# Rotary embedding in a two-layer streaming encoder: tables scaled by the norm, and another order of the mixing steps

## The reference, cut to what matters

```python
def rmsnorm(x, g):
    xf = x.astype(jnp.float32)
    y = xf * lax.rsqrt(jnp.mean(xf * xf, axis=-1, keepdims=True) + EPS)
    return (y * g.astype(jnp.float32)).astype(x.dtype)

def rope(x, pos):
    ...
    x1, x2 = xf[..., :half], xf[..., half:]
    return jnp.concatenate([x1 * cos - x2 * sin, x2 * cos + x1 * sin], axis=-1).astype(x.dtype)

def token_mix(z, pos, ws, bs, sink, g_q, w_uq, w_uk, w_uv, g_kv, cache):
    u, va, q, k, vb, cq, ckv_raw, kpe_raw = split_proj(z)
    q = rope(q.reshape(B, T, B_HEADS, B_HEAD_DIM), pos)
    k = rope(k.reshape(B, T, B_KV_HEADS, B_HEAD_DIM), pos)
    ...
    b = swa_prompt(q, k, vb, sink)
    c_lat = mla_prompt(q_lat, q_pe, ckv, kpe)

def layer(h, pos, cache, ...):
    h = ffn_half(h, n1, w1g, w1u, w1d)
    z = rmsnorm(h, nm) @ w_in
    m, st = token_mix(z, pos, ...)
    h = h + m @ w_out
    h = ffn_half(h, n2, w2g, w2u, w2d)
```

## Time and profile before

| | us |
|---|---|
| median of 3 runs (2272.84 to 2275.41) | 2273.33 |
| the profiled execution, its own time | 2275.03 |
| span of the profiled execution | 2273.0 |
| busy in the span: PE, DVE, ACT, POOL | 2214.6, 693.7, 676.1, 755.9 |
| mixing of the first layer, from `z:v` to the last output step | 454 to 696 |
| mixing of the second layer, the same stretch | 1573.6 to 1815.6 |

### The profile page before, as it was taken

How to read it: one execution, slowest core, us unless ns; L and a number is a source line. 1 busy time by engine, 2 the same in 40 slices (tenths; PEclk the granted TensorE clock), 3 DMA queues, 4 the chain that set the end, 5 groups by cost and what they waited for, 6 DMA issues and landing times.

```text
span 2273.0 us, 41807 instructions
## 1 busy us (share of the span) xinstructions
PE 2214.6 (97%) x16519; PEld 2147.2 (94%) x16519; DVE 693.7 (31%) x993; ACT 676.1 (30%) x1074; POOL 755.9 (33%) x324
## 2 busy tenths in 40 slices
PE   8999999998998999999999999999989999999999
PEld 7999999997778999999999999999977799999999
DVE  5222211146646222221122222112555462222211
ACT  5222222224434222222232222222244342222222
POOL 3334343431022433343433433334311133333331
PEclk9999999999998999999999999999999999999999
DMA  4322222331111323223222232324211022322232
GB/s 121 91 75 83 83 86 77 105 88 41 51 47 38 93 74 92 74 79 92 80 76 82 77 89 74 93 76 119 61 45 53 29 75 74 92 74 87 75 91 86
DMA packets 344052, 176.16 MB, mean 77 GB/s; under 512 B 36848, under 2 KB 339152, under 8 KB 343952
## 3 DMA queue, kind: packets, MB, share of 16 engines
q1 hardware_dynamic: 341872, 171.15, 26.5%
q10 hardware_dynamic: 2080, 3.67, 0.5%
HBM read 171.17 MB, written 3.62 MB: 77 GB/s over the span
## 4 chain that ended last, share of the span: by engine, by line
PE 91%; DVE 5%; issue 2%; ACT 2%; DMA 0%; SPq 0%; DVEq 0%; ACTq 0%
PE pair L879 85%; DVE sq_sum L1193 1%; PE pair L1071 1%; PE pair L1057 1%; PE pair L1079 1%; PE pair L1011 1%; DVE top L1379 1%; PE pair L1049 1%; PE pair L1062 0%; ACT probs L785 0%; DVE rms_q L1327 0%; DVE rms_kv L1321 0%; PE pair L1094 0%; DMA raw<-in_w_up_dram 0%; PE pair L896 0%
## 5 line engine op out<-in xcount | busy, mean ns | idle before, releaser
L618 POOL TENSOR_TENSOR w_low<-raw,w_high 128x1024 fp32r<-128x1024 f32 (+1 forms) x320 | 755.7, 2379 | 1489.2 <-ACT w_high L643 1489.2
L879 PE MATMUL pair<-x_high,w_high 128*128 128x288 f32 x3296 | 712.1, 298 | 4.7 <-DVE h L1435 2.8
L879 PE MATMUL pair<-x_low,w_high 128*128 128x288 f32 x3296 | 707.6, 296 | 0.0
L879 PE MATMUL pair<-x_high,w_low 128*128 128x288 f32 x3296 | 707.4, 296 | 0.0
L879 PEld LDWEIGHTS pair<-x_high,w_high 128*128 128x128 f32 x3296 | 533.1, 189 | 8.2 <-DVE x_low L1187 3.0
L879 PEld LDWEIGHTS pair<-x_low,w_high 128*128 128x128 f32 x3296 | 533.0, 189 | 0.0
L879 PEld LDWEIGHTS pair<-x_high,w_low 128*128 128x128 f32 x3296 | 532.8, 189 | 0.0
L643 ACT ACTIVATE w_high<-raw 128x1024 fp32r<-128x1024 f32 (+1 forms) x322 | 318.3, 1023 | 233.6 <-DMA raw<-in_w_down_dram 151.1
L879 PE MATMUL pair<-hidden_high,w_high 128*128 128x288 f32 x1408 | 301.6, 296 | 0.0
L879 PE MATMUL pair<-hidden_low,w_high 128*128 128x288 f32 x1408 | 301.5, 296 | 0.0
L879 PE MATMUL pair<-hidden_high,w_low 128*128 128x288 f32 x1408 | 301.4, 296 | 0.0
(11 more groups left out here) (183 smaller groups left out, 1377.0 us busy)
## 6 DMA issues: line engine op xcount, KB each, us to landing
raw<-in_w_up_dram SPq DMA_DIRECT2D x90, 512.0 KB, 3.8
raw<-in_w_gate_dram SPq DMA_DIRECT2D x88, 512.0 KB, 4.1
raw<-in_w_down_dram SPq DMA_DIRECT2D x64, 512.0 KB, 3.6
raw<-in_w_down_dram SPq DMA_DIRECT2D x32, 384.0 KB, 3.3
raw<-in_w_in_dram SPq DMA_DIRECT2D x20, 512.0 KB, 3.9
raw<-in_w_in_dram SPq DMA_DIRECT2D x16, 256.0 KB, 3.6
raw<-in_w_out_dram SPq DMA_DIRECT2D x8, 512.0 KB, 3.7
raw<-in_w_out_dram SPq DMA_DIRECT2D x16, 256.0 KB, 3.9
```

The source lines that it names most:

```text
L618: nc.gpsimd.tensor_tensor(**low_of(s, slot_size(s))).then_inc(low_ready, 1)
L879: mm = nc.tensor.matmul(ps[p][:, half, 0:HALF], w, x[:, half * HALF:(half + 1) * HALF], start=first and k == 0 and q == 0, stop=last and k ...
```

## The change

The norm and the rotary tables are both factors for each position, so they are multiplied with each other once a layer: `sin64` and `cos64` become sin x rms and cos x rms, in place, in the DVE part of `z:k`. A rotated tile then takes three passes: z = PSUM x sin64 (what the half swap reads), dst = PSUM x cos64, and, behind the half swap on PE, dst = PSUM + dst. The multiplication by sin goes ahead of the half swap, which is right since both halves of a head have the same sines. The PSUM pair of a rotated projection is now emptied by two passes.

`PLAN` is another list: the same steps in another order, with other pairs. The buffer of `probsT` is now taken by the step's turn in the list (`buffer_of`), which in this list gives each step the buffer that its number gave before.

```diff
-PLAN = """w:q0 z:k@0 sumx@3 w:q1 z:v@1 tw@2 w:q2 z:q0@0 w:q3 w:va0 w:va1 rot:k@3 tc@2 z:q1@1 rot:q0@3 z:q2@0 rot:q1@3 tv@1
...
+PLAN = """w:q0 z:k@0 sumx@3 w:q1 z:v@1 tw@2 w:q2 z:q0@0 w:q3 w:va0 rot:k@2 w:va1 tc@1 rot:q0@3 w:u0 z:q1@0 tv@3 z:q2@2
...
-    n = {"z": 1, "sumx": 1, "sumkv": 2, "sumq": 1, "tw": 1, "rot": 3, "a": 4, "qp": 1, "qn": 1,
+    n = {"z": 4 if arg == "k" else 2 if step in ROTATED else 1, "sumx": 1, "sumkv": 2, "sumq": 1, "tw": 1, "rot": 3 if arg in ("kpe", "qp") else 1, "a": 4, "qp": 1, "qn": 1,
...
 def evacuated(step):
 
     kind, arg = split(step)
+    if step in ROTATED:
+        return "vector", vector_end(step)
...
+def buffer_of(step):
+
+    kind, arg = split(step)
+    turn = [s for s in MIX if split(s)[0] in ("T", "MT")]
+    return turn.index({"T": "T", "O": "T", "MT": "MT", "MO": "MT"}[kind] + f":{arg}") % 2
...
                             nc.vector.reciprocal(rms[:, :], rms[:, :]).then_inc(rms_ready, 1)
                             dve.wait_ge(rms_ready, 3 * layer + 2)
+                            dve.wait_ge(mix_in, layer * N_MIX_IN + MIX_IN_FIRST)
+                            emit(nc.vector.tensor_tensor(sin64[:, :], sin64[:, :], rms[:, :], ALU.mult), names[0])
+                            emit(nc.vector.tensor_tensor(cos64[:, :], cos64[:, :], rms[:, :], ALU.mult), names[1])
+                            own(names[1])
...
-                        emit(nc.vector.tensor_tensor(rows2(dst), halves(p), rows2(rms), ALU.mult), names[0])
+                        if step in ROTATED:
+                            emit(nc.vector.tensor_tensor(rows2(dst), halves(p), rows2(sin64), ALU.mult), names[-2])
+                            emit(nc.vector.tensor_tensor(rows2(roped[arg]), halves(p), rows2(cos64), ALU.mult), names[-1])
+                        else:
+                            emit(nc.vector.tensor_tensor(rows2(dst), halves(p), rows2(rms), ALU.mult), names[0])
...
+                        if arg in roped:
+                            pe_did(dve, layer, step)
+                            own(vector_end(f"z:{arg}"))
+                            emit(nc.vector.tensor_tensor(rows2(roped[arg]), halves(p), rows2(roped[arg]), ALU.add), names[0])
+                            continue
```

More of the change, by code:

```diff
@@ L103 @@
 MLA_TILES = [1, 3, 4, 2, 0]
-PLAN = """w:q0 z:k@0 sumx@3 w:q1 z:v@1 tw@2 w:q2 z:q0@0 w:q3 w:va0 w:va1 rot:k@3 tc@2 z:q1@1 rot:q0@3 z:q2@0 rot:q1@3 tv@1
[L105 to L112, removed]
+PLAN = """w:q0 z:k@0 sumx@3 w:q1 z:v@1 tw@2 w:q2 z:q0@0 w:q3 w:va0 rot:k@2 w:va1 tc@1 rot:q0@3 w:u0 z:q1@0 tv@3 z:q2@2
+rot:q1@1 z:q3@0 rot:q2@2 z:va0@1 w:u1 w:ckv w:cq0 rot:q3@2 z:va1@1 tva:0@2 S:0@3 z:u0@0 T:0@1 w:cq1 tva:1@2 S:1@3
+z:u1@0 tk@2 a:0@1 T:1@3 O:0@0 S:2@2 z:ckv@3 a:1@2 w:cq2 w:kpe T:2@3 S:3@2 z:cq0@0 O:1@0 T:3@1 S:4@3 sumkv@2 O:2@3
+T:4@0 S:5@1 z:cq1@2 z:cq2@3 O:3@2 T:5@0 w:qn w:A0 S:6@1 z:kpe@3 sumq@2 vc:0@0 O:4@3 T:6@0 rep@1 S:7@2 tckv@1 qp@3
+rot:kpe@0 O:5@2 T:7@3 S:8@0 tkpe@1 qn:0@2 O:6@3 A:0@0 w:A1 T:8@2 w:B0 S:9@1 qn:1@3 A:2@2 O:7@0 T:9@1 ql:0@3
+ql:1@2 O:9@0 A:5@1 rot:qp@0 A:1@2 vc:1@1 O:8@0 w:B1 ql:2@2 MS:0@1 ql:3@0 A:7@3 A:6@2 A:3@0 MT:0@2 MS:1@1 MO:0@3
+w:B2 B:0@0 MT:1@1 MS:2@3 B:2@0 A:4@2 MT:2@1 MS:3@0 MO:2@3 B:1@1 B:3@0 MO:1@3 MT:3@2 MS:4@1 MO:3@3 B:4@2 MT:4@3
+MS:5@1 w:B3 B:5@2 w:C0 MT:5@3 MS:6@1 w:C1 B:6@2 MO:4@1 MT:6@0 MS:7@3 B:7@1 MO:5@3 MT:7@0 MS:8@2 MO:6@0 MT:8@1
+MS:9@3 MO:8@1 MO:7@0 MT:9@3 MO:9@1""".split()
 MIX = [t.partition("@")[0] for t in PLAN]
@@ L191, with vector_end @@
 DVE_STEPS = [x for s in MIX for x in vector_ops(s)]
+def vector_end(step):
+    return vector_ops(step)[-1]
 def evacuated(step):
     kind, arg = split(step)
+    if step in ROTATED:
+        return "vector", vector_end(step)
     if kind in ("z", "qp", "qn", "O", "MO", "A", "B"):
         return "vector", f"{step}.0"
-    if kind in ("rot", "a"):
+    if kind == "rot":
+        return "vector", f"{step}.1" if arg in ("kpe", "qp") else f"{step}.0"
+    if kind == "a":
         return "vector", f"{step}.1"
     return "scalar", scalar_ops(step)[-1]
+def buffer_of(step):
+    kind, arg = split(step)
+    turn = [s for s in MIX if split(s)[0] in ("T", "MT")]
+    return turn.index({"T": "T", "O": "T", "MT": "MT", "MO": "MT"}[kind] + f":{arg}") % 2
 def before_in_pair(step):
@@ L236, in tensor_needs @@
         "sumq": lambda: ["z:cq2.2"],
-        "rot": lambda: [] if arg == "kpe" else ["qp.0" if arg == "qp" else f"z:{arg}.0"],
+        "rot": lambda: [] if arg == "kpe" else ["qp.0" if arg == "qp" else vector_ops(f"z:{arg}")[-2]],
         "rep": lambda: ["z:kpe.0"],
         "tv": lambda: ["z:v.0"],
-        "tk": lambda: ["rot:k.2"],
+        "tk": lambda: [vector_end("rot:k")],
         "tckv": lambda: ["sumkv.1"],
@@ L248, in tensor_needs @@
         "ql": lambda: [f"qn:{arg // 2}.0"],
-        "S": lambda: ["rot:k.2"] + [f"rot:q{2 * swa_unit(arg)[1] + e}.2" for e in range(2)],
+        "S": lambda: [vector_end("rot:k")] + [vector_end(f"rot:q{2 * swa_unit(arg)[1] + e}") for e in range(2)],
         "MS": lambda: ["rot:qp.2", "rot:kpe.2", "sumkv.1"],
@@ L1333, in mixing @@
                     elif kind == "rot":
[L1334 to L1339, removed]
+                        if arg in roped:
[3 more added lines that the diff above has]
+                            continue
+                        src, dst, cos, sin = {"kpe": kpe_rep, "qp": zs[1]}[arg], {"kpe": kpeT, "qp": qpT}[arg], cos32, sin32
+                        if arg == "qp":
+                            own("qp.0")
                         else:
```

8 lines of the change are left out of this document (5 added, 3 removed).

## The result

The changed kernel took 2285.1 us in the median of 6 runs (2274.3 to 2286.9) against 2273.3 before, a ratio of 1.0043 with an interval of 1.0024 to 1.0062, which is 5.5 to 14.1 us. By the medians it is 12 us slower; 8 were forecast.

A forecast was written before the change was run, and what follows sets the result against it. PE, busy 97% of the span, was taken as the bound. A layer: waits 17.2, gaps 0.3 and clock 2.1 make 19.6 us, less 15.6 gone: 4.0 more, 8.1 in two, so 2281.4 us; range 2267 to 2290.

The forecast's parts named there:

- The walk: Mixing stage from 454 on: the new list followed step by step with known durations, giving 4.0 us more a layer.
- `z:q0`: Query projection on PE: waits 0.8 us until pair 0 is emptied, behind the two table products.
- `O:1`: Output step on PE: waits 3.6 us for DVE to empty the pair of z:cq0 behind the chain of S:3.
- `O:2`: Output step on PE: waits 3.6 us for the exponentials of S:4, whose pair it uses.
- `T:9`: Transposes on PE behind the chain of S:9: wait 1.55 us.
- The first three meetings: Small DVE score steps in S:3, S:6 and S:9 held by a POOL w_low: 1.6, 1.45 and 1.9 us.
- `T:6`: Transposes on PE, in the pair of vc:0: wait 0.8 us for its copy.
- 2.1 for two lowered stretches, less 1.6: PE clock lowered behind the waits of O:1 and O:2, 2.1 us a layer, against 1.6 gone.
- the idle term: PE waits a layer: 17.2 us new, with 14.0 us of today's idle time gone.
- rival (3): Clock lowered behind T:6 and T:7 too, each 1.5 us: 6 us more, 2287.4; chance 0.14.
- Rival (1): The three meetings with w_low don't happen: 4.6 us back a layer, 0.6 a layer faster than before, 2272; chance 0.28.
- that of `S:6`, 1.3: Chain of S:6: 1.3 us a layer given back if its meeting with w_low doesn't happen.

The follow-up runs named there:

- short_low: The changed kernel with POOL making only 64 columns of the w_low of cq2, kpe, qn, A0 and B0, part of the work left out; 2271.5 us.
- old_q0: The kernel before with three passes, scaled tables and its old list, but z:q0 in pair 3 and rot:k in pair 0; 2275.3 us.
- old_passes: The changed kernel's new list of steps and pairs, with the four passes and unscaled tables of the kernel before; 2281.5 us.
- old_order: The changed kernel's three passes and scaled tables, with the list of steps and pairs of the kernel before; 2278.5 us.
- again: The changed kernel run and profiled once more, unchanged; 2285.3 us, ratio 1.0051 to the kernel before.
- hold_low: The changed kernel with all work done, but POOL waiting for score steps of S:3, S:6 and S:9 before five w_low; 2273.8 us.

## Why the prediction was right, and where it was off

**The walk held.** Of its waits, most came within 0.3 us: `z:q0` 0.69 (0.8, where its own times give 0.7), `O:1` 3.37 (3.6), `O:2` 3.40 (3.6), `T:4` 0.75 (0.8), `T:7` 1.7 (1.7), `O:5` 0.6 (0.45), `T:9` 1.71 (1.55), `O:4` 0.95 (1.1). The first three meetings were where it put them, at 1.50 and 0.3 more on `neg_max`, 1.68 and 2.27 us for 1.6, 1.45 and 1.9. `T:6` waited 0.2, not 0.8; it had 0.98 in short_low, where `O:4` ahead of it has no wait. The tail's waits were 4.5, not 3.84. The rotation's last pass takes 0.76 us, and busy DVE fell from 693.7 to 691.8. Idle time rose by 2.7 and 2.9 a layer where the walk gave 3.5. (The terms of its sum give 8.0 for two layers, not 8.1.)

**The passes are worth nothing, but not free.** old_q0 and old_passes show that no shorter rotation reaches PE. The cost of 0.8 us at `z:q0` was right as a wait and short as a price: it came to 2.9 to 3.2 us in both layers (old_order against old_q0), with the clock that went with it. That the price beyond the wait is clock was argued from busy times of single executions, not shown by itself.

**The clock was mis-sized.** The term "2.1 for two lowered stretches, less 1.6" gave 0.5 us more a layer; measured are 1.8 and 3.6. So the idle term was 0.6 to 0.8 too high and the clock term 1.3 to 3.1 too low, and part of the nearness of 8 to 12 is that these errors have opposite signs. Both stretches came where they were put (548 and 558). Not foreseen was a third, twice as long, behind `T:9` at 619.6. In the run again it stands behind `T:7` and not at 619. The window behind `T:7` in the first profile, and then in again:

```profile
602.00:612.00 10.00, 9.38 (x93) 8.08 (x93) 6.67 (x14) 5.30 (x17) 2.72 (x2) 1.00 0.01 2
```

```profile
602.00:612.00 10.00, 9.49 (x59) 8.21 (x59) 5.33 (x12) 4.37 (x14) 0.17 (x1) 0.66 0.01 2
```

So the same waits don't fix the place of a stretch. In return the stretch in the tail is 3.4 us long, not 10.2, which wasn't foreseen either. The time lies between the forecast and rival (3), with 2287.4, whose stretch behind `T:7` is the one in the run again.

**Rival (1) was near in its time, not in its terms.** It said 2272 without the meetings; short_low took 2271.5 and hold_low 2273.8. So the meetings make nearly all of the loss: without them the time is that of the kernel before within 2 us. But it gave back 9.2 us, and 11.3 to 13.6 came back, and of its three terms that of `S:6`, 1.3, is worth next to nothing on PE: in the first layer `O:4` and `T:6` wait 1.1 together with the meeting, 1.4 in hold_low and 1.0 in short_low without it. Against the run again the two stages of hold_low are 9.6 us shorter, 6.9 of it idle time and 2.7 busy time of the same instructions, which is clock; against the changed kernel's first profile these are 8.3 and 1.5.

The Trainium skill, SBUF — State Buffer, section "Who interferes with whom", lets the engine that issued first hold the shared pair for its whole instruction. The runs agree: in hold_low `den_all` ends at 543.73 and the `w_low` ahead of it at 543.70. The prediction read the earlier trace rows as ending with the `w_low`, too. It doesn't: the pass ends at 489.77, the `w_low` at 489.15, so the pass is held until then and does most of its own work behind it, which a step of four numbers a partition doesn't show. The Trainium skill, SBUF — State Buffer, section "Summary: rules for kernel authors", advises to schedule whichever is off the critical path; POOL's wait does that here.

**Shares.** The three passes cost 4.8 us with the old list and 3.8 with the new one, the order 7.8 with the old passes and 6.8 with the new ones. Both shares taken alone add up to 12.6, against 11.6 for the change in the same job; the intervals, 4 us wide and more, don't tell the difference from nothing.

## What to carry to other kernels

Where a chain of DVE steps with two SBUF inputs is on the critical path and POOL reads SBUF beside it, a large POOL step should start when DVE begins to wait for another engine, and a semaphore wait on POOL puts it there; moving the copy that feeds it only moved the meeting within the chain of `S:3`. Look also at what waits behind the chain: the meeting in `S:6` cost PE next to nothing. Price each new wait of PE with its clock, by the busy time of the same instructions at both levels, and fill a wait that can't be removed with matmuls measured to be shorter than it. Here the passes hidden behind PE won nothing when they went, but a pass put between PSUM and the next user of its pair cost at once.
